# Three products of 256 columns for each weight tile, summed in one PSUM region, in a two-block fp32 transformer kernel

## The reference

```python
z = rms_norm(h, g) @ w_in                               # 2048 -> 4656
kc = gelu(blocks(k_c) @ cmp_w1_k) @ cmp_w2_k            # 60 columns, K = 2048
h = h + rms_norm(y @ w_out, g)
h = h + rms_norm(square(relu(rms_norm(h, g) @ mlp_w1)) @ mlp_w2, g)
h = h + sigmoid(h @ ple_gate) * (p @ ple_proj)
...
y = (silu(gate) * up) @ w_ffn_out                       # both layers of the second model
```

## Time and profile before

| | before |
|---|---|
| median of 3 runs | 4117.04 us |
| span of the profiled execution | 4127.4 us |
| TensorE, matrix products | 3762.5 us busy, 91% of the span, 21616 instructions |
| TensorE, weight loads (PEld) | 3236.9 us, 78%, 21616 instructions |
| VectorE | 2405.3 us, 58% |
| ScalarE | 1980.2 us, 48% |
| GpSimd | 713.8 us, 17% |
| mean DMA rate | 150 GB/s |
| granted TensorE clock, mean | 0.924 |

### The profile page before, as it was taken

One profiled execution on the slowest core, in us unless ns is written; L12 is line 12 of the kernel. 1 busy time (PEld: TensorE's weight loads), 2 busy tenths in 40 slices (PEclk: granted clock), 3 DMA queues, 4 the chain that ended last, 5 costly groups with the idle time before them and its releaser, 6 DMA issues.

```text
span 4127.4 us, 64496 instructions
## 1 busy us (share of the span) xinstructions
PE 3762.5 (91%) x21616; PEld 3236.9 (78%) x21616; DVE 2405.3 (58%) x4056; ACT 1980.2 (48%) x2811; POOL 713.8 (17%) x835
## 2 busy tenths in 40 slices
PE   6999989999997899859899999978647989999997
PEld 5887768888886788748688888868646868888886
DVE  4665565555555455555655555765995565555556
ACT  3465444444444644534575444543214667544444
POOL 1000330111125300034300001070001130000107
PEclk9997989999998999979899999985658989999999
DMA  6550435555553455403355555550002535555555
GB/s 164 178 193 22 136 123 189 183 186 187 184 187 125 155 173 190 152 1 133 123 188 188 183 188 194 179 193 1 2 1 92 188 125 186 188 182 187 186 185 177
DMA packets 177283, 618.28 MB, mean 150 GB/s; under 512 B 18758, under 2 KB 29576, under 8 KB 176920
## 3 DMA queue, kind: packets, MB, share of 16 engines
q1 hardware_dynamic: 167424, 604.05, 43.6%
q10 hardware_dynamic: 9752, 12.81, 1.4%
HBM read 611.54 MB, written 5.24 MB: 149 GB/s over the span
## 4 chain that ended last, share of the span: by engine, by line
PE 83%; DVE 9%; POOL 3%; ACT 2%; issue 2%; ACTq 1%; DMA 0%; DVEq 0%; POOLq 0%
PE bank L1288 51%; PE bank L1289 25%; DVE prod L1097 3%; POOL res L1149 2%; DVE st L1102 2%; DVE st L1100 2%; PE m L1607 1%; PE m L1335 1%; POOL act L1144 1%; DVE rstd L701 1%; PE m L1574 0%; PE m L1548 0%; PE m L1413 0%; ACT w_hi L341 0%; PE m L1624 0%
## 5 line engine op out<-in xcount | busy, mean ns | idle before, releaser
L1288 PE MATMUL bank<-act,w_hi 128*128 128x512 f32 x6528 | 2345.0, 403 | 38.6 <-POOL act L1144 35.7
L692 DVE TENSOR_TENSOR w_lo<-w_raw,w_hi 128x1024 fp32r<-128x1024 f32 x1148 | 1417.7, 1253 | 1000.2 <-ACT w_hi L341 980.1
L1289 PE MATMUL bank<-act,w_lo 128*128 128x256 f32 x6528 | 1846.8, 283 | 0.0
L1288 PEld LDWEIGHTS bank<-act,w_hi 128*128 128x128 f32 x6528 | 1238.6, 190 | 368.2 <-issue 39.2
L341 ACT ACTIVATE w_hi<-w_raw 128x1024 fp32r<-128x1024 f32 x1148 | 1190.3, 1055 | 405.6 <-PE bank L1289 400.0
L1289 PEld LDWEIGHTS bank<-act,w_lo 128*128 128x128 f32 x6528 | 1251.1, 192 | 0.1
L1288 PE MATMUL bank<-ffn,w_hi 128*128 128x512 f32 x2432 | 859.8, 399 | 0.0
L1289 PE MATMUL bank<-ffn,w_lo 128*128 128x256 f32 x2432 | 683.0, 281 | 0.0
L345 ACT ACTIVATE low<-bank 128x256 f32<-128x256 f32 x572 | 219.1, 383 | 890.8 <-PE bank L1289 890.5
L1288 PEld LDWEIGHTS bank<-ffn,w_hi 128*128 128x128 f32 x2432 | 457.0, 188 | 114.1
L1289 PEld LDWEIGHTS bank<-ffn,w_lo 128*128 128x128 f32 x2432 | 459.4, 189 | 0.0
(11 more groups left out here) (283 smaller groups left out, 2311.9 us busy)
## 6 DMA issues: line engine op xcount, KB each, us to landing
w_raw<-stream SPq DMA_DIRECT2D x1148, 512.0 KB, 3.3
toeplitz<-rel_rows ACTq DMA_DIRECT2D x1, 3072.0 KB, 32.5
res<-x_t ACTq DMA_DIRECT2D x4, 512.0 KB, 10.1
bias<-toeplitz ACTq DMA_DIRECT2D x1, 2048.0 KB, 10.7
out<-res SPq DMA_DIRECT2D x4, 512.0 KB, 2.8
bias<-toeplitz ACTq DMA_DIRECT2D x1, 1024.0 KB, 13.3
b_raw<-s_b ACTq DMA_DIRECT2D x1, 1024.0 KB, 7.0
c_raw<-s_c ACTq DMA_DIRECT2D x1, 1024.0 KB, 4.7
```

What stands on the lines that cost most here:

```text
L692: e.tensor_tensor(w_lo[:, q, :], w_raw[:, q, :], w_hi[:, q, :].bitcast(F32), ALU.subtract).then_inc(lo_ready, 1)
L1288: mm(bank[w][:, 0:2 * n], w_hi[:, q, wt], x(h * hk + k, 0, 2 * n), start=(h == 0 and k == 0), stop=False)
L1289: last = mm(bank[w][:, n:2 * n], w_lo[:, q, wt], x(h * hk + k, 0, n), start=False, stop=(h == 1 and k == hk - 1))
```

## The change

In `unit`, the 512-column product becomes two of 256 columns, and all three products of a weight tile go to columns 0 to n-1 of the bank. The second half of the bank is no longer used there. `copy_low` goes away on ScalarE in every phase but proj. `drain` becomes a copy from PSUM on VectorE that waits for the products themselves. In proj the count it waits for starts at zero, since no other phase counts there any more.

```diff
-        def copy_low(i, w, n=T):
-            s.wait_ge(halves_used, 4 * i + (2 * w + 2))
-            a(low[:, w, 0:n], bank[w][:, n:2 * n], ACT.Copy).then_inc(low_copied, 1)
+        def nothing(i, w):
+            pass
...
-            run_phase(s, "in1", hi, copy_low, behind=lru_behind)
+            run_phase(s, "in1", hi, nothing, behind=lru_behind)
...
         def drain(i, w, dst, n=T):
-            v.wait_ge(low_copied, 2 * i + (w + 1))
-            e.tensor_tensor(dst, bank[w][:, 0:n], low[:, w, 0:n], ALU.add).then_inc(drained, 1)
+            v.wait_ge(halves_used, 4 * i + (2 * w + 2))
+            e.tensor_copy(dst, bank[w][:, 0:n]).then_inc(drained, 1)
...
                 if mt % 8 == 7:
-                    v.wait_ge(low_copied, 2 * i0 + mt // 8 + 1)
+                    v.wait_ge(low_copied, mt // 8 + 1)
...
-                    mm(bank[w][:, 0:2 * n], w_hi[:, q, wt], x(h * hk + k, 0, 2 * n), start=(h == 0 and k == 0), stop=False)
-                    last = mm(bank[w][:, n:2 * n], w_lo[:, q, wt], x(h * hk + k, 0, n), start=False,
+                    mm(bank[w][:, 0:n], w_hi[:, q, wt], x(h * hk + k, 0, n), start=(h == 0 and k == 0), stop=False)
+                    mm(bank[w][:, 0:n], w_hi[:, q, wt], x(h * hk + k, n, 2 * n), start=False, stop=False)
+                    last = mm(bank[w][:, 0:n], w_lo[:, q, wt], x(h * hk + k, 0, n), start=False,
                               stop=(h == 1 and k == hk - 1))
```

More of the change, by code:

```diff
@@ L431, in cmp_low @@
             def cmp_low(i, w):
-                copy_low(i, w, 60)
                 s.wait_ge(drained, 2 * i + w + 1)
@@ L482, in _ @@
                 a(act[:, 8 + k, 0:T], z[:, 24 + k, :], ACT.Copy).then_inc(act_hi, 1)
-            run_phase(s, "out1", hi, copy_low)
+            run_phase(s, "out1", hi, nothing)
             norm("post1", y, DT, sq, D, None)
         def up1_low(i, w):
-            copy_low(i, w)
             s.wait_ge(f_val, 2 * (i - cur[1]) + (w + cur[2] + 1))
@@ L506, in feed_forward @@
                     run_phase(s, up, hi, up_low, behind=s5_behind if s_ == "ffn0" and g == 2 and "s5" in plan else None)
-                    run_phase(s, down, hi, copy_low)
+                    run_phase(s, down, hi, nothing)
             norm("post_" + name, y, DT, sq, D, None)
@@ L558, in _ @@
             act_high("in2", sq, scaled_ready("in2"))
-            run_phase(s, "in2", hi, copy_low)
+            run_phase(s, "in2", hi, nothing)
             s.wait_ge(drained, 2 * PH["in2"][1])
@@ L628, in _ @@
                 a(act[:, 8 + k, 0:T], z[:, 8 + k, :], ACT.Copy).then_inc(act_hi, 1)
-            run_phase(s, "out2", hi, copy_low)
+            run_phase(s, "out2", hi, nothing)
             norm("post2", y, DT, sq, D, None)
```

## The result

The changed kernel takes 4199.63 us (median of four runs, 4195.1 to 4209.9) where the one before takes 4114.32 us on the same chip: ratio 1.0192, 95% interval 1.0165 to 1.0219, so some 79 us slower (the two medians lie 85.3 us apart, inside that interval). The range of 4050 to 4215 held it, and slower was the side with the most chance, but the case that I forecast, next to no change, was wrong. The profiled execution has a span of 4193.3 us, 65.9 more than the profiled one of before, less than the timed runs show. Measured in the two traces from the first to the last w_hi product of each of the ten product phases, those phases are 81 us longer in sum, 13.4 of it in cmp, and the stretches between them are 15 us shorter.

A forecast was written before the change was run, and what follows sets the result against it. TensorE, busy 91%, was taken to bound the kernel through the pace of its product pairs. Bulk -15.9, cmp +13.7 and joins -4.2 gave -6.4 us from 4117.0, so 4110.5 us, range 4050 to 4215.

The forecast's parts named there:

- The bulk: Pairs outside cmp: a triple costs 3 x 116.7 = 350 ns at both paces, -15.9 us; bounds -113 and +140 us.
- Rival E: Loads back to back become the bound in the product stream: triple 360 ns, total +81 us, 4198 us; chance 0.14.
- rival C: Every product and load pays the surplus, 13.3 or 16.7 ns: triple 360 or 370 ns, 4267 us; chance 0.10.
- B: At the slow pace the long product's excess moves to the triple: 357 and 350 ns, +38.6 us, 4156 us; chance 0.25.
- D: The short step shrinks to 113 ns, as for the transposes: -113 us in the bulk, 4014 us; chance 0.10.
- A third weight load: In the products of a weight tile: the two w_hi loads are not merged, so a triple has three loads.
- Load hidden: In the product stream: the load runs during the preceding 256-column product, so the step is 0.12 us despite a 0.19 load.
- rival F: The w_hi load is exposed (5787 us, chance 0.01) or merged (4097 us, chance 0.02); chance 0.03 in all.
- cmp: In the cmp phase loads set the pace at clock 0.50: a third load adds 64 x 213.5 ns, +13.7 us.
- Joins: At ten phase ends the shorter drain starts VectorE 0.42 us earlier (cmp 0.26): -4.2 us, bounds -4 to -6.
- Steady state: Within phases, removing 572 ScalarE copies, some 220 us, is worth nothing, as ScalarE is busy 48% and runs ahead.
- A: The forecast case: the short step of 116.7 ns holds for all three products, 4110 us (4095 to 4125); chance 0.38.

The follow-up runs named there:

- e1: Changed kernel with the MLP groups' three products per weight tile at other widths, 128 to 512 columns, same load; steps 111 ns at 192 to 226 at 512.
- e6: Products of the kernel before with the changed drain: VectorE copies the first half, ScalarE copies nothing; ratio 0.9985 (0.9962 to 1.0009).
- e2: Changed kernel with narrower weight loads (64 or 32 columns) in MLP groups, some with other product widths or pairs; 256 columns with 32 took 113 ns.
- e3: Changed kernel with unequal w_hi and w_lo products in the MLP groups, such as 512+256 (352 ns a pair) and 512+64 (340 ns).

## Why the prediction was wrong, point by point

**The step that failed** is "The bulk", where I took 350 ns for a triple as three times the short step of before. It measured 360: by the same counts of pairs +72 us in place of -15.9. The mis-sized term is what a product more costs, 13.3 ns at the quick pace and not 3.3. Half splitting (355.5) and whole splitting (360, with one region or with two) put the loss on the third product with its load. The row was right and the reading wrong: the start of a product after a long one comes late and after a short one early, by 3.3 ns at the quick pace (230 + 116.7 where 226.7 + 120 are due). I noted that the quick pace fits a straight line with 3.3 ns a product. Two points always fit a line; the other split, equal surplus for each product (26.7/2), fitted the pair's sum as well, and only e1 has more points. It lies within the upper bound that I gave, and I chose between the ends by the row that looked the most alike.

**Rival E gave the number and not the cause.** It said 360 ns and 4198 us, and 4199.63 was measured. But its mechanism, the load as the bound at 256 columns, is refuted: the load's floor is 112 ns, and 512 columns still pay 13.3. What the runs show is rival C's at its lower value, at both paces; C's 16.7 at the slow pace was wrong, since the slow pace was seen in streams with a product of 512 columns in them and not with three of 256 and full loads. C's rule is no law either: it holds here for full loads and 256 or at least 320 columns. Rivals B (moved excess) and D (113) are refuted, D's 113 only appears with at most half the load's width.

**A third weight load:** right, 30640 products and 30640 loads. **Load hidden:** right, and never exposed at 256 columns. The Trainium skill, "TensorE: Matmul & The Clock Gate", section "The mechanism", has the sentence by which the prediction's rival F would expose it ("only when row_grp differs"), but the same section also lets a load that goes to the background weight buffer pass products in flight, which the prediction left out. The trace agrees with the second: e1 shows 720 loads and 720 products of 272 columns in 90 us, 125 ns a step. **cmp:** right, +13.7 forecast, 41.0 against 27.3 us measured, clock at 0.50. **Joins:** right in size at the join shown (0.4 us), too small to be timed. The sum was written as -4.2 where nine joins of 0.42 and cmp's 0.26 make -4.0. **Steady state:** right, ScalarE's 188 us less bought nothing that e6 could measure. **Phase starts, waits, DMA:** no cost appeared there; 11 of the 15 us by which the stretches between the product phases are shorter in the changed kernel's profile stay unexplained, and are of the size by which two executions of the kernel before differ. **The range:** its lower end, 4050, was said to lie halfway between A and D, which is 4062; the result doesn't hang on it.

**The paces:** I said that the trace can't tell their cause and still used them as properties of phases, 2020 and 6770 pairs. They are states that vary from run to run, and even within a phase. The sum of 82 us uses the shares of one execution; with all stages quick before it would be 127 us, with all slow 68. That the measured 79 is near 82 owes something to luck in these shares.

**What stays open:** why a product with its load pays 13.3 ns, whether the product or the load causes it (loads of 64 columns halve it at 128 and 256 columns of the product and not at 384 or 512), and what puts a stage into the slow pace. No product without its own load was tried.

## What to carry to other kernels

A split of a product in equal parts with the same weights is a weight load more for each part added; here that is 13.3 ns on a pair of 347, some 4%, and moving a copy off an engine with time to spare (ScalarE, 48% busy) gains only at the joins. Price a stream of products by the sum over a whole period of it, never by the step of one product in it, and get at least three sizes before splitting a surplus into a fixed part and a slope. Where products are small, as in cmp with 60 columns, count loads and not columns.

## What the runs showed of the hardware

With fp32r operands and a clock of 1.00 (2.4 GHz), the step of products with a 128-column load each was 120.0 ns at 256 columns, 146 at 320, 173 at 384 and 226 at 512, which is the columns plus 13.3 to within 1 ns. At 272 and 288 columns it was 125 and 131, less than that. It didn't fall below 111 to 112 at 192, 224 and 240 columns. With 64 columns of weights it did fall, to 60 ns at 128 columns (e2). At a clock of 0.50 (1.2 GHz) the step was 213.5 ns in cmp and 213 with 128 columns in e1, the time of 256 columns at that clock with no surplus beyond it. The Trainium skill, "TensorE: Matmul & The Clock Gate", section "LDWEIGHTS (loading the stationary operand)", gives P/1.2 ns for a load of P columns, by which 128 columns are an estimated 107. The trace is near it at a clock of 1.00 (112) and at twice that at 0.50. Products of 512 and 256 columns in turn have two paces, 346.7 and 353.4 ns a pair, that mostly last for a whole stage and fall differently in each execution. Between long products, a short one of 64 columns costs as much as one of 128: 340 and 338 ns a pair (e3).
